# Which engine sends for the bias tables in the second mixer: GpSimd, or SyncE between its weight loads

## The chip, the cores and the metric

One core of one Trainium2 chip runs the kernel in one launch. The metric is the device time in microseconds (us), the median of several runs. Five engines work side by side, each in its own program order: TensorE (PE) multiplies, VectorE (DVE), ScalarE (ACT) and GpSimd (POOL) do elementwise work, and SyncE (SP) here only issues DMAs. They wait for one another through semaphores. A DMA is issued by an instruction in one engine's program; the bytes are moved by the core's 16 DMA engines, and the DMA's semaphore rises when they have landed.

## The reference

Two transformer blocks run one after the other on x of 512 tokens by 1024 channels, all float32. The first has causal pooling, a dilated attention and a gated MLP. The second begins with the part that matters here, a mixer with 14 attention heads of three kinds, whose scores get a bias before the softmax:

```python
# differential attention: 4 heads, two score maps each, ALiBi bias
s = jnp.einsum('bqhd,bkhd->bhqk', qb, k).astype(jnp.float32) * scale + bias      # bias = -slope * |qpos - kpos|
# forgetting attention: 6 heads, causal mask only
# chunk attention: 6 heads, a relative-position bias looked up in a table
s = jnp.einsum('bcqhd,bckhd->bchqk', qc, kb).astype(jnp.float32) * (HEAD_DIM ** -0.5) + bias
```

After the mixer come an output projection, a convolution-gated MLP and a gated embedding step.

## The kernel before, in words

Every float32 product is made of three products of rounded parts: hi times hi, lo times hi, hi times lo. For each load of weights ACT therefore writes `w_hi` and POOL or DVE writes `w_lo` from `w_raw`. The buffers `w_raw`, `w_hi` and `w_lo` have two slots; load n goes to the slot of load n-2, so SP issues it once the `w_lo` of load n-2 is complete.

Mixer two works through 11 chunks of the projection: three of two forgetting heads, three of two chunk heads (`chk`), four of one differential head (`d`), one of the differential values (`dv`). A chunk has two loads, so there are 22, numbered 0 to 21 (`load_projection`, L920). A load of a `chk` chunk is 3 DMAs, one of a `d` chunk 4, one of `dv` 1. While the PE projects one chunk, it attends to the chunk before: for each map m (20 maps; 8 to 13 are forgetting heads, 14 to 19 chunk heads, 0 to 7 differential) and each query tile t from 3 down to 0, the PE forms scores ("S", L2506/L2507), DVE adds the table row, takes the maximum and returns the bank (L1876, semaphore `biased`), ACT takes the exponential (L1306), POOL normalises ("N", L1061), PE transposes ("T", L2518), ACT and DVE split the result (L1313, L1957), and PE multiplies by the values ("PV", L2528/L2530). Between these lie, for each chunk and token tile, "sum" (POOL, L991/L992: the inverse root of the sum of squares), "rows" (DVE, L1813/L1820: scale by it, and return the projection's bank), and "turn" (PE transposes of the finished rows, L2470; then ACT L1289 and L1295 and DVE L1831 write the ring of queries and keys). A planner writes all these steps into one order with small shifts for each engine; each engine then keeps its own order (`mx.orders["pool"]`, L1031). The eight PSUM banks are four for projections and four that S, T, PV and turn take in rotation; a step waits until the one four before it in the rotation has been read.

The bias tables: ten of 128x512 float32, 256 KB each, in two buffers `tables[:, i % 2, :]`. Table i with i from 0 to 5 serves map 14+i, tables 6 to 9 serve the pairs of differential maps. Tables 0 and 1 are sent for by POOL at L1176, after its part of the norm between the blocks. Tables 2 to 9 are steps "table" in POOL's order: POOL waits until the last map that read this buffer is done (`biased`) and issues the DMA (L1068). For the first six, half of the last 64 columns has to be set to minus 1e30 by POOL: for i from 2 to 5 this is a step "mask" (L1072), two units of scores after the step "table":

```python
elif kind == "mask":
    i = s[1]
    pool.wait_ge(table_in[i % 2], 16 * (i // 2 + 1))
    pool.memset(tables[0:HD, i % 2, S - HD:S], MASKED).then_inc(table_masked, 1)
```

The order that the planner gives POOL around table 3 (the first number of a sum is its chunk, the second its token tile; of N the map and its tile):

```
... sum(5,0)  TABLE 3  N(16,3)  sum(5,1)  N(16,2)  sum(5,2)  MASK 3  N(16,1)  sum(5,3)  w_lo of load 13  N(16,0)  TABLE 4 ...
```

DVE's `rows(5,3)` waits for POOL's `sum(5,3)`, and PE's two turns of chunk 5 wait for `rows(5,3)`.

Of the kernel before, what the change touches and what calls it, by code (L numbers as in the profile page):

```python
# [55 lines left out]
def round_done(j, k=SEVEN):  # L56


    return SEVEN * j + (k - 2)
# [270 lines left out]
def two_blocks_kernel(nc, A, out):  # L330
# [23 lines left out]
    G_MIX2 = G_DOWN1 + T * N_DOWN  # L354
# [10 lines left out]
    mixers = []  # L365
    for b, (cnt, steps, chunks, units, c0, norm) in enumerate(((n1, steps1, chunks1, units1, 0, 0),
                                                               (n2, steps2, chunks2, units2, C_MIX2, 2))):
        m = Mixer()
# [9 lines left out]
        for k, chunk in enumerate(chunks):  # L378
            for half in range(1 if chunk[0] == "pool" else 2):
                m.load_at[k, half] = len(m.loads)  # L380
                m.loads.append((k, KH * half, KB if chunk[0] == "pool" else KH))
                last = ("poolproj", k, 1, POOL_PARTS - 1) if chunk[0] == "pool" else ("proj", k, half, T - 1)
# [86 lines left out]
    def table_of_map(m):  # L469

        return 6 + m // 2 if m < 8 else None if m < 14 else m - 14
# [13 lines left out]
    with ExitStack() as ctx:  # L485
# [3 lines left out]
        def sem(name):  # L489
            return ctx.enter_context(nc.semaphore(name))  # L490
# [34 lines left out]
        def at(name, kib, shape, dt=F32):  # L525

            assert kib * KIB + int(np.prod(shape[1:])) * 4 <= arena_kib * KIB, name
            return nc.alloc_sbuf_tensor_at(name, shape, dt, offset=arena_start + int(kib * KIB))
# [57 lines left out]
        tables = at("tables", 44, [P, 2, S])  # L586
# [7 lines left out]
        table_in = [sem("table_in0"), sem("table_in1")]  # L594
# [7 lines left out]
        products_done = sem("products_done")  # L602
# [24 lines left out]
        biased = sem("biased")  # L627
# [175 lines left out]
        def projection_weights(mx, n):  # L803

            k, kb0, kbs = mx.loads[n]
            slot, wide = (mx.c0 + n) % 2, width(mx.chunks[k])
            return [w[:, slot, 0:kbs * wide].rearrange("p (k n) -> p k n", n=wide) for w in (w_raw, w_hi, w_lo)]
# [47 lines left out]
        def _(sp):  # L855
# [26 lines left out]
            def out_chunks(w, c0, b):  # L882
                for j, c in enumerate(OUT_ORDER[b]):
                    load(c0 + j, (c0 + j) % 2, rows(w)[c], rows=True)
# [35 lines left out]
            def load_projection(mx, n):  # L920
                c, (k, kb0, kbs) = mx.c0 + n, mx.loads[n]
                w = A["w_in_2" if mx.b else "w_in"][0].rearrange("(k p) n -> p k n", p=P)[:, kb0:kb0 + kbs, :]
                dst = projection_weights(mx, n)[0]
                if c >= 2:
                    sp.wait_ge(lo_done, 4 * (c - 1))
                at_ = 0
                for col, wide in columns(mx.chunks[k]):
                    sp.dma_start(dst[:, :, at_:at_ + wide], w[:, :, col:col + wide]).then_inc(raw_in[c % 2], 16)
                    at_ += wide

            def const(dst, src, **kw):
                sp.dma_start(dst, src, **kw).then_inc(const_in, 16)

# [20 lines left out]
            for n in range(2, len(mixers[0].loads)):  # L954
# [2 lines left out]
            blocks(A["w_gate"][0], A["w_up"][0])  # L957
            row_chunks(A["w_down"][0], C_DOWN1,
                       [[(piece_lo, round_done(N_BLOCK - 2 + e)), (w_sums, 4 * (N_BLOCK - 1 + e))] for e in range(2)])
            for n in range(len(mixers[1].loads)):  # L960
                load_projection(mixers[1], n)
            out_chunks(A["w_out_2"][0], C_OUT2, 1)
            mixed_pairs(A["w_up_2"][0], C_UP2)
            row_chunks(A["w_down_2"][0], C_DOWN2, [[(gate_w_lo, gate_pieces_done(N_MIXED - 1, 3))], [(val_w_lo, 4 * N_MIXED)]])
# [16 lines left out]
        def _(pool):  # L981
# [8 lines left out]
            def rstd(out_, mean):  # L990
                link(pool.tensor_scalar(mean, mean, EPS, None, ALU.add))  # L991
                return pool.tensor_tensor(out_, mean, half_neg[:, 0:out_.shape[-1]], ALU.pow)  # L992
# [36 lines left out]
            def mixer(mx):  # L1029
                own_n, own_d = mx.cnt.of[mx.steps[0]]["N"], 0  # L1030
                for s in mx.orders["pool"]:  # L1031
                    kind, of = s[0], mx.cnt.of[s]
                    own_n, own_d = own_n + (kind == "N"), own_d + (kind == "pool_d")
                    if kind == "split_lo":
                        weights_lo(mx, s[1], s[2])
                    elif kind == "sum":
                        r = of["sum"]
                        pool.wait_ge(ss_done, r + 1)
                        rstd(qk_rs[:, r % 4, :], qk_ss[:, r % 4, :]).then_inc(rs_done, 1)
                    elif kind == "combine":  # L1040
                        pool.wait_ge(combine_ss, s[1] + 1)
                        pool.tensor_tensor(rs_c[:, :], den_c[:, :], half_neg[:, :], ALU.pow).then_inc(combine_rs, 1)
                    elif kind == "zeros":
                        pool.wait_ge(h_turned, T * (mx.norm + 1))
                        pool.wait_ge(x_squared, T * (mx.norm + 1))
                        for half in range(2):
                            for i in range(2):
                                ins = pool.memset(ring[:, 6 * half + 3 * i + 2, :].bitcast(F32), 0.0)
                        ins.then_inc(zeros_set, 1)
                    elif kind == "N2":  # L1050
                        h, t = s[1:]
                        u, col = mx.unit[2 * h, t], sum_column(h, t)
                        ratio = rden[:, u % 8:u % 8 + 1]
                        pool.wait_ge(second_rden, of["N2"] + 1)
                        pool.tensor_scalar(ratio, ratio, den_d[:, col:col + 1], lam[:, 2:3], ALU.mult, ALU.mult)\
                            .then_inc(ratio_done, 1)
                    elif kind == "N":
                        u, kn = mx.unit[s[1:]], P * (s[2] + 1)
                        pool.wait_ge(rden_done, of["N"] + 1)
                        p = prob[:, u % NPROB, 0:kn]  # L1060
                        pool.tensor_tensor(p, p, rden[:, u % 8:u % 8 + 1].to_broadcast([P, kn]), ALU.mult)\  # L1061
                            .then_inc(normed, 1)
                    elif kind == "table":
                        i = s[1]
                        last = max(mx.unit[m, 0] for m in range(20) if table_of_map(m) == i - 2)
                        pool.wait_ge(biased, last + 1)
                        table = A["rel_table"][:, i, :] if i < 6 else A["alibi"][:, i - 6, :]
                        pool.dma_start(tables[:, i % 2, :], table).then_inc(table_in[i % 2], 16)  # L1068
                    elif kind == "mask":
                        i = s[1]  # L1070
                        pool.wait_ge(table_in[i % 2], 16 * (i // 2 + 1))
                        pool.memset(tables[0:HD, i % 2, S - HD:S], MASKED).then_inc(table_masked, 1)  # L1072
                    elif kind in ("widen", "mean", "pool_d"):
                        m = s[1]
                        u, d, spare = pool_u[:, m, :], pool_d[:, m, :], (pool_d[:, 1, :], pool_u[:, 0, :])[m]
                        if kind == "widen":
                            j = s[2]
                            dst, src = (spare, d)[j % 2], (u, spare, d, spare)[j]
                            if j == 0:
                                k = mx.chunks.index(("pool",))  # L1080
                                pool.wait_ge(bank_read, mx.cnt.of["poolproj", k, m, POOL_PARTS - 1]["bank"] + 1)
                                if m:
                                    pool.wait_ge(pool_out, m)
                            sh = 1 << j
                            link(pool.tensor_copy(dst[:, 0:sh], src[:, 0:sh]))
                            link(pool.tensor_tensor(dst[:, sh:S], src[:, sh:S], src[:, 0:S - sh], ALU.add))
                        elif kind == "mean":
                            lo, win = HD * s[2], 2 << (2 * m + s[2])
                            src = (spare, d)[s[2]]
                            pool.wait_ge(normed, own_n)  # L1090
                            if own_d:
                                pool.wait_ge(pool_out, own_d)
                            pool.wait_ge(lo_done, lo_split[0])
                            link(pool.tensor_tensor(d[lo:lo + HD, 0:16], src[lo:lo + HD, 0:16],
                                                    pool_inv[lo:lo + HD, m, :], ALU.mult))
                            link(pool.tensor_scalar(d[lo:lo + HD, 16:S], src[lo:lo + HD, 16:S], 1.0 / win, None, ALU.mult))
                        else:
                            pool.tensor_tensor(d, d, u, ALU.subtract).then_inc(pool_out, 1)
# [73 lines left out]
                    block_sums(2 * i + e, e)  # L1172
            norm(2, True)

            for i in range(2):
                pool.dma_start(tables[:, i, :], A["rel_table"][:, i, :]).then_inc(table_in[i], 16)  # L1176
            pool.dma_start(causal[:, :], A["causal"]).then_inc(causal_in, 16)
            pool.memset(ft[:, :].bitcast(F32), 0.0).then_inc(ft_zeroed, 1)
            pool.memset(ones[:, :], 1.0)
# [1673 lines left out]
```

## Time and profile before

| | us |
|---|---|
| median of 3 runs | 1303.28 (1303.08 to 1303.86) |
| the profiled execution, its own time | 1302.76 |
| its span, first to last instruction | 1301.0 |
| PE busy | 1279.9 (98%) |
| DVE / ACT / POOL busy | 863.7 / 682.8 / 474.9 |

The span is what the trace covers; the profiled execution's time is 1.76 us more. Busy time is the sum of instruction durations. The idle time before an instruction, and what released it, stand in brackets at its end in the timelines. Mixer two lies between about 577 and 850 us of the span.

### The profile page before, as it was taken

What the parts mean: (1) busy time and instruction counts of PE and PEld (TensorE: products, weight loads), DVE (VectorE), ACT (ScalarE), POOL (GpSimd) and SP (SyncE); (2) the same over time, 40 slices, a digit from 0 to 9 for tenths busy, and PEclk for the clock granted to TensorE, in tenths of its full rate; (3) what the DMA queues carried; (4) which work ended last, traced back from release to release, by engine and by line L of the source; (5) the groups of instructions that cost most, each with busy time, mean ns of one, the idle gap of its engine ahead of it and who ended that gap; (6) DMA issues with size and microseconds to landing.
All of it is one profiled execution on the core that took longest, in us unless ns stands there. A gap on an engine that the chain in (4) does not pass through costs nothing. (4 is left out here: it accounts for less than half of the span.)

```text
span 1301.0 us, 21929 instructions
## 1 busy us (share of the span) xinstructions
PE 1279.9 (98%) x7792; PEld 1162.3 (89%) x7792; DVE 863.7 (66%) x1584; ACT 682.8 (52%) x1361; POOL 474.9 (37%) x546
## 2 busy tenths in 40 slices
PE   8999999999999999999999999999999999999998
PEld 6999988999999988889999988889888989888887
DVE  4677766799888733374666778557977777633454
ACT  4666745445555522256667678435455546422352
POOL 5565681256555300027766756210122232000000
PEclk9999999999999999999999999999999999999999
DMA  6312213233322332223222332232223232422221
GB/s 195 87 52 80 90 42 129 77 119 108 119 97 97 119 108 97 89 62 86 74 65 50 72 68 89 91 115 83 97 82 114 81 113 65 172 95 97 72 98 65
DMA packets 120639, 120.64 MB, mean 93 GB/s; under 512 B 22732, under 2 KB 107419, under 8 KB 120562
## 3 DMA queue, kind: packets, MB, share of 16 engines
q1 hardware_dynamic: 118464, 112.92, 27.5%
q0 software_dynamic: 2096, 6.71, 1.6%
q8 instruction: 46, 0.75, 0.2%
q14 instruction: 31, 0.25, 0.1%
q10 hardware_dynamic: 2, 0.00, 0.0%
HBM read 117.52 MB, written 2.10 MB: 92 GB/s over the span
## 5 line engine op out<-in xcount | busy, mean ns | idle before, releaser
L2337 PE MATMUL ps<-h_hi,w_hi 128*128 128x256 f32 (+1 forms) x752 | 239.1, 318 | 0.4 <-ACT ps L1578 0.4
L2338 PE MATMUL ps<-h_lo,w_hi 128*128 128x256 f32 (+1 forms) x752 | 238.5, 317 | 0.0
L2339 PE MATMUL ps<-h_hi,w_lo 128*128 128x256 f32 (+1 forms) x752 | 238.3, 317 | 0.0
L1714 DVE TENSOR_TENSOR w_lo<-w_raw,w_hi 128x512 fp32r<-128x512 f32 x164 | 105.8, 692 | 143.5 <-ACT w_hi L1217 143.4
L1217 ACT ACTIVATE w_hi<-w_raw 128x512 fp32r<-128x512 f32 x164 | 92.4, 620 | 176.7 <-PE ps L2560 153.3
L2556 PE MATMUL ps<-w_hi,st_hi 128*128 128x512 f32 x432 | 169.1, 391 | 0.0
L2423 PE MATMUL ps<-w_hi,h_hi 128*128 128x384 f32 (+2 forms) x528 | 167.9, 328 | 0.6 <-DVE work L1813 0.3
L2560 PE MATMUL ps<-w_hi,st_lo 128*128 128x512 f32 x432 | 168.2, 389 | 0.0
L2558 PE MATMUL ps<-w_lo,st_hi 128*128 128x512 f32 x432 | 168.2, 389 | 0.0
L2425 PE MATMUL ps<-w_hi,h_lo 128*128 128x384 f32 (+2 forms) x528 | 163.3, 319 | 0.0
L2339 PEld LDWEIGHTS ps<-h_hi,w_lo 128*128 128x128 f32 x752 | 143.3, 191 | 9.6
L2337 PEld LDWEIGHTS ps<-h_hi,w_hi 128*128 128x128 f32 x752 | 143.3, 191 | 9.5 <-ACT ps L1578 0.6
L2338 PEld LDWEIGHTS ps<-h_lo,w_hi 128*128 128x128 f32 x752 | 143.4, 191 | 8.5
L1026 POOL TENSOR_TENSOR w_lo<-w_raw,w_hi 128x384 fp32r<-128x384 f32 (+2 forms) x116 | 115.8, 1018 | 48.7 <-ACT w_hi L1229 45.8
L2430 PE MATMUL ps<-w_lo,h_hi 128*128 128x384 f32 (+2 forms) x528 | 105.0, 320 | 0.5 <-POOL w_lo L1026 0.5
L2423 PEld LDWEIGHTS ps<-w_hi,h_hi 128*128 128x128 f32 x528 | 99.5, 188 | 3.1 <-issue 1.1
L2425 PEld LDWEIGHTS ps<-w_hi,h_lo 128*128 128x128 f32 x528 | 99.7, 189 | 0.8
L2337 PE MATMUL ps<-t_hi,w_hi 128*128 128x256 f32 x344 | 97.5, 283 | 1.8 <-DVE hid L2064 0.9
L2339 PE MATMUL ps<-t_hi,w_lo 128*128 128x256 f32 x344 | 97.4, 283 | 0.0
L2338 PE MATMUL ps<-t_lo,w_hi 128*128 128x256 f32 x344 | 97.3, 283 | 0.0
L2560 PEld LDWEIGHTS ps<-w_hi,st_lo 128*128 128x128 f32 x432 | 81.1, 188 | 16.9
L2556 PEld LDWEIGHTS ps<-w_hi,st_hi 128*128 128x128 f32 x432 | 81.1, 188 | 16.8 <-DVE h_lo L1751 0.3
(264 smaller groups left out, 2899.3 us busy)
## 6 DMA issues: line engine op xcount, KB each, us to landing
w_raw<-in_w_up_dram SPq DMA_DIRECT2D x25, 1024.0 KB, 5.2
w_raw<-in_w_down_dram SPq DMA_DIRECT2D x22, 1024.0 KB, 4.8
w_raw<-in_w_in_dram SPq DMA_DIRECT2D x72, 256.0 KB, 3.4
w_raw<-in_w_gate_dram SPq DMA_DIRECT2D x11, 1024.0 KB, 5.2
w_raw<-in_w_out_dram SPq DMA_DIRECT2D x8, 1024.0 KB, 4.8
w_raw<-in_w_up_dram SPq DMA_DIRECT2D x16, 512.0 KB, 3.5
w_raw<-in_w_in_dram SPq DMA_DIRECT2D x32, 128.0 KB, 2.9
w_raw<-in_w_ple_gate_dram SPq DMA_DIRECT2D x4, 1024.0 KB, 5.0
```

The costliest lines, as they stand in the source:

```text
L1026: pool.tensor_tensor(w_lo[:, c % 2, q], w_raw[:, c % 2, q], w_hi[:, c % 2, q].bitcast(F32), ALU.subtract)\
L1217: act.activation(w_hi[:, slot, q], w_raw[:, slot, q], ACT.Copy).then_inc(hi_done, 1)
L1714: dve.tensor_tensor(w_lo[:, slot, q], w_raw[:, slot, q], w_hi[:, slot, q].bitcast(F32), ALU.subtract).then_inc(lo_done, 1)
L2337: pe.matmul(out_, s_hi, m_hi, start=first and n == 0, stop=False, skip_group_check=True)
L2338: pe.matmul(out_, s_hi, m_lo, start=False, stop=False, skip_group_check=True)
L2339: mm = pe.matmul(out_, s_lo, m_hi, start=False, stop=last and n == len(pairs) - 1, skip_group_check=True)
L2423: pe.matmul(bank, h_hi[:, kb0 + i, tok], hi[:, i, :], start=half == 0 and i == 0, stop=False, skip_group_check=True)
L2425: pe.matmul(bank, h_lo[:, kb0 + i, tok], hi[:, i, :], start=False, stop=False, skip_group_check=True)
L2430: mm = pe.matmul(bank, h_hi[:, kb0 + i, tok], lo[:, i, :], start=False, stop=half == 1 and i == KH - 1, skip_group_check=True)
L2556: pe.matmul(bank, rows_hi[:, k, tok], hi[:, k, col], start=first and k == 0, stop=False, skip_group_check=True)
L2558: pe.matmul(bank, rows_hi[:, k, tok], lo[:, k, col], start=False, stop=False, skip_group_check=True)
L2560: mm = pe.matmul(bank, rows_lo[:, k, tok], hi[:, k, col], start=False, stop=last and k == RB - 1, skip_group_check=True)
```

## The change

The ten DMAs for the tables leave POOL's program and go into SP's. A new function `loads_and_tables` writes one order for SP out of POOL's order: load 0, load 1, table 0, table 1, load 2, load 3, and then, walking through POOL's steps, each table where POOL had it, and each load n where POOL begins the last of its own pieces of `w_lo` of load n-2. Written out this gives: loads 4 to 13, T2, load 14, T3, load 15, T4, load 16, T5, load 17, T6, load 18, T7, load 19, load 20, T8, load 21, T9, and then the loads of the output projection. Tables 0 and 1 now wait on SP for the last product of block one (`products_done`, `G_MIX2`), the others for the same counts of `biased` as before. The masks, their place and their waits stay on POOL.

```diff
+            def loads_and_tables(mx):
+                order = [("load", 0), ("load", 1), ("table", 0), ("table", 1), ("load", 2), ("load", 3)]
+                for s in mx.orders["pool"]:
+                    if s[0] == "table":
+                        order.append(s)
+                    elif s[0] == "split_lo" and s[2] == (1 if ("split_rest", s[1], 1) in mx.cnt.of else 3) \
+                            and 2 <= s[1] < len(mx.loads) - 2:
+                        order.append(("load", s[1] + 2))
+                return order
+
+            def load_table(mx, i):
+                if i < 2:
+                    sp.wait_ge(products_done, G_MIX2)
+                else:
+                    last = max(mx.unit[m, 0] for m in range(20) if table_of_map(m) == i - 2)
+                    sp.wait_ge(biased, last + 1)
+                table = A["rel_table"][:, i, :] if i < 6 else A["alibi"][:, i - 6, :]
+                sp.dma_start(tables[:, i % 2, :], table).then_inc(table_in[i % 2], 16)
...
-            for n in range(len(mixers[1].loads)):
-                load_projection(mixers[1], n)
+            for kind, n in loads_and_tables(mixers[1]):
+                if kind == "load":
+                    load_projection(mixers[1], n)
+                else:
+                    load_table(mixers[1], n)
...
-                    elif kind == "table":
-                        i = s[1]
-                        last = max(mx.unit[m, 0] for m in range(20) if table_of_map(m) == i - 2)
-                        pool.wait_ge(biased, last + 1)
-                        table = A["rel_table"][:, i, :] if i < 6 else A["alibi"][:, i - 6, :]
-                        pool.dma_start(tables[:, i % 2, :], table).then_inc(table_in[i % 2], 16)
...
-            for i in range(2):
-                pool.dma_start(tables[:, i, :], A["rel_table"][:, i, :]).then_inc(table_in[i], 16)
```

## Rows read from the trace of the kernel before

**Rows 1.** The page: busy time, share and instructions of each engine, and the span.

```profile
span 1301.0 us, 21929 instructions
...
PE 1279.9 (98%) x7792; PEld 1162.3 (89%) x7792; DVE 863.7 (66%) x1584; ACT 682.8 (52%) x1361; POOL 474.9 (37%) x546
```

**Rows 2.** PE by stretches: length, PE busy (instructions), clock, DMA share, GB/s.

```profile
700.00:722.00 22.00, 21.52 (x136) 1.00 0.19 48
722.00:742.00 20.00, 18.41 (x141) 1.00 0.31 67
742.00:840.00 98.00, 93.95 (x701) 1.00 0.31 90
sum 250.00, PE 242.63; mean PE 60.66
```

**Rows 3.** Instructions on the tile tables: duration min/median/max ns, starts; time to landing.

```profile
L1068 POOL DMA_DIRECT2D tables<-in_rel_table_dram x4: 622/626/639, 706.1 to 743.9; - x4
L1176 POOL DMA_DIRECT2D tables<-in_rel_table_dram x2: 538/586/633, 586.1 to 586.8; - x2
...
DMA to landing us min/median/max: 3.1/3.4/4.3
```

**Rows 4.** SP's issues of projection loads in order of time: start, length, count.

```profile
574.20 1.47 SPq L928 DMA_DIRECT2D w_raw<-in_w_in_dram  x3
...
706.21 2.88 SPq L928 DMA_DIRECT2D w_raw<-in_w_in_dram  x4
722.01 2.92 SPq L928 DMA_DIRECT2D w_raw<-in_w_in_dram  x4
731.67 2.02 SPq L928 DMA_DIRECT2D w_raw<-in_w_in_dram  x4
744.13 2.06 SPq L928 DMA_DIRECT2D w_raw<-in_w_in_dram  x4
```

**Rows 5.** Line 928 from 700 to 800 us: its issues' durations, and time to landing.

```profile
L928 SPq DMA_DIRECT2D w_raw<-in_w_in_dram x30: 367/507/1412, 706.2 to 793.5; - x30
...
DMA to landing us min/median/max: 2.3/3.0/3.8
```

**Rows 6.** POOL in order of time around tables 2 to 5 and their masks.

```profile
713.95 0.14 POOL L1072 MEMSET tables<- 64x64 f32 x1
...
718.19 0.63 POOL L1068 DMA_DIRECT2D tables<-in_rel_table_dram  x1
...
724.71 1.04 POOL L992 TENSOR_TENSOR qk_rs<-qk_ss,half_neg 128x4 f32<-128x4 f32 x1
725.70 0.14 POOL L1072 MEMSET tables<- 64x64 f32 x1
...
726.82 1.04 POOL L992 TENSOR_TENSOR qk_rs<-qk_ss,half_neg 128x4 f32<-128x4 f32 x1
...
738.25 0.14 POOL L1072 MEMSET tables<- 64x64 f32 x1
...
749.28 0.14 POOL L1072 MEMSET tables<- 64x64 f32 x1
```

**Rows 7.** DVE in order of time, from rows(5,3) to the last ring of chunk 5.

```profile
727.96 0.42 DVE L1813 TENSOR_TENSOR work<-ps,qk_rs 128x256 f32<-128x256 f32 x1 [0.55 <-POOL qk_rs L992]
...
728.50 0.68 DVE L1876 CUSTOM_DVE_ANT_0 prob<-ps,tables 128x512 f32<-128x512 f32 x1
...
734.35 1.51 DVE L1831 SCALAR_TENSOR_TENSOR ring<-ps,gcol,ring 64x512 fp32r<-64x512 f32 x2 [1.21 <-ACT ring L1289]
```

**Rows 8.** ACT in the same stretch.

```profile
730.01 0.71 ACT L1306 ACTIVATE prob<-prob,neg_max 128x512 f32<-128x512 f32 x1
730.62 0.19 ACT L1306 ACTIVATION_READ_ACCUMULATOR prob<-prob,neg_max 128x1 f32 x1
730.84 1.39 ACT L1289 ACTIVATE ring<-ps,gcol 64x512 fp32r<-64x512 f32 x2
```

**Rows 9.** PE: the turns of chunk 5, and the wait for their ring.

```profile
729.31 1.25 PE L2470 MATMUL ps<-ident,work 128*128 128x128 f32 x8
...
735.92 0.38 PE L2506 MATMUL ps<-ring 128*128 128x256 f32 x1 [1.59 <-DVE ring L1831]
```

**Rows 10.** The start of mixer two: PE's last product of block one; ACT's split of load 2.

```profile
577.48 0.39 PE L2560 MATMUL ps<-w_hi,st_lo 128*128 128x512 f32 x1
...
594.31 1.58 ACT L1229 ACTIVATE w_hi<-w_raw 128x768 fp32r<-128x768 f32 x2 [2.93 <-PE ps L2430]
```

**Rows 11.** From 700 to 840 us, PE's and DVE's waits: total us, times, longest.

```profile
PE ps L2470 <- DVE neg_max L1876: 1.7, 3, 0.6
...
DVE w_lo L1911 <- POOL w_lo L1026: 3.2, 3, 2.0
...
DVE work L1813 <- POOL qk_rs L992: 1.6, 3, 0.6
```

**Rows 12.** Around table 9: the last read of its buffer (DVE), SP's next load.

```profile
800.10 0.29 DVE L1876 CUSTOM_DVE_ANT_0 prob<-ps,tables 128x128 f32<-128x128 f32 x1
...
803.21 0.37 SPq L861 DMA_DIRECT2D w_raw<-in_w_out_dram  x1
```

## The prediction

> **What bounds the kernel now.** I read the page first. PE is busy for 1279.9 of 1301.0 us, POOL for 37% [rows 1]; so an instruction taken off POOL is worth something only where PE stands still because POOL is late. Second, PE by stretches over mixer two: from 590 to 840 us it is busy 242.63 of 250 us, so 7.4 us stand still, and 1.59 of them between 722 and 742 [rows 2]. Third, PE's waits from 700 to 840 us, where tables 2 to 9 are sent for. None names POOL. The largest kind with a pattern, 1.7 us in three pieces, is a turn that waits for DVE to return a bank [rows 11]. DVE for its part waits for POOL, 1.6 us for inverse roots and 3.2 us for `w_lo` [rows 11]. That is the only road by which a faster POOL could reach PE, and equally the road by which a late POOL reaches it. Fourth, the instructions on the tables, which give the price on POOL and the time to landing [rows 3]. Last, SP's issues in order of time [rows 4], because the change makes each table wait behind a load.
>
> **The change part by part.**
>
> *POOL loses ten issues.* Eight at L1068 of 0.626 us make 5.0 us, two at L1176 make 1.17 us [rows 3]. They lie beside other work. The two early ones are followed by POOL work that DVE's first sums do not wait for; of the eight, only DVE's 4.8 us of waits for POOL could shrink [rows 11], and PE's own waits in that stretch name DVE's bank returns and rings, not anything that POOL is late with. Bounds for PE: nothing, or at most the 1.6 us of waits for inverse roots. I take nothing.
>
> *SP gains ten issues.* One DMA takes 0.37 to 0.51 us to issue there [rows 5]. The next load starts at least 7 us after a projection load's issues end (724.93 to 731.67 is the shortest of the gaps in [rows 4]), so they fit. I take nothing.
>
> *SP gains ten waits; what is queued behind each?* Tables 0 and 1 wait for the last product of block one, which ends at 577.87 [rows 10]. Load 2 stood at 574.20 [rows 4] and now follows them: 577.9 plus two issues of 0.5 is 578.9, 4.7 us later; with 1.5 us of issues and 3.8 us to land it is there by 584.2. ACT reads it at 594.31, and is held there by PE [rows 10]: 10 us of cover. Tables 2 to 7 wait for `biased` counts that are reached well before the load ahead of them in the queue has gone. Table 9 waits for the unit that DVE finishes at 800.10 plus 0.29; the load behind it goes at 803.21 [rows 12], so 2.4 us of cover after the issue. All at nothing.
>
> *The tables come at another time.* This is where I find a price. The new order puts table i behind a load whose own wait may end later than POOL's turn for that table:
>
> - Table 2: behind load 13, whose issues end at 706.21 + 2.88 = 709.09 [rows 4]. Landing at 3.1 us, the least of the tables' rows [rows 3], is 712.2, at 3.8 us [rows 5] 712.9. POOL's mask stands at 713.95 [rows 6]: hidden by 1.0 us.
> - Table 3: POOL sent for it at 718.19 [rows 6]. Load 14, now ahead of it, waits until 722.01 and its four issues end at 724.93 [rows 4]. The table is issued 6.7 us later than before, and lands at 724.93 + 3.1 = 728.03. POOL comes to its mask at 725.70 [rows 6]. It now waits until about 728.05: **2.35 us late**.
> - Table 4: behind load 15, 731.67 + 2.02 = 733.69 [rows 4], landed by 736.8 to 737.5, mask at 738.25 [rows 6]: hidden by 0.8 us. The delay below moves both sides by similar amounts.
> - Table 5: behind load 16, 744.13 + 2.06 = 746.19 [rows 4], landed by 749.3 to 750.0, mask at 749.28 [rows 6], or 0.6 us sooner without POOL's issue: POOL stands for 0.6 to 1.3 us. Behind this mask come only a normalisation and `w_lo` pieces of load 15, which are needed several steps later, and no "sum"; the sum of the last tile is ahead of it in POOL's order. I take nothing, at most 0.5.
> - Tables 6 to 9 have no mask, and each is sent for many units of scores before its first use. Nothing.
>
> *Table 3's 2.35 us, followed on.* Behind the mask on POOL are N(16,1) and sum(5,3), whose root ended at 726.82 + 1.04 = 727.86 and will end at 730.2 [rows 6]. DVE's rows(5,3) at 727.96 had already waited 0.55 us for it [rows 7], so DVE is late by the whole 2.35 us: rows(5,3) ends at 730.7, and PE's turn, at 729.31 before [rows 9], starts 1.4 us late. DVE next adds the table for S(17,3), now from 730.85 to 731.53 instead of 728.50 to 729.18 [rows 7]. ACT's exponential waits for it, so 730.01 becomes 731.55. Exponential and accumulator took until 730.81, and ACT began the ring at 730.84 [rows 8]; now that is 732.38, 1.54 us later. The ring is ACT's and then DVE's chain (DVE had waited 1.21 us for ACT in it [rows 7]), and PE's S(17,1) at 735.92 had stood 1.59 us for its end [rows 9]. So the wait is not cover: it is the end of the same chain, and PE resumes 1.54 us later. Roughly, PE loses the mask's delay less 0.8 us.
>
> **The sum.** 8 + 2 issues off POOL: 0. SP's waits: 0. Table 3: +1.5. The span becomes 1302.5, and that execution's time 1302.76 + 1.5 = 1304.3. The median of the runs shown is 0.5 us above the profiled time, so I forecast 1303.28 + 1.5 = 1304.8. PE has almost no later gaps in which to win it back.
>
> Bounds of the unknown, the landing of a table issued by SP, which this trace does not have: 2.3 us, the least of L928 [rows 5], gives a mask delay of 1.55 and a loss of 0.75; 4.3 us, the most of the tables [rows 3], gives 3.55 and 2.75. I take 3.1, the same bytes at the nearest shape. Load 14's issues, too, had one of 1.4 us where 0.5 is usual [rows 4, 5]; if that hiccup goes, 0.9 us comes off.
>
> The rows show 3.1 us to landing even for a table that POOL sent for [rows 3]. The Trainium skill, "DMA: Bandwidth & Descriptors", section "Latency and other measured facts", puts the first byte at about 0.6 us for a DMA from the synchronising engine and about 1 us for one from GpSimd. By that the table would land 0.4 us sooner after its issue, and the loss would be about 1.1 instead of 1.5; no row here sets the two paths side by side for the same transfer. The same page, section "Two DMAs through the same engine are not ordered", says that descriptors within one queue start in order. That speaks against this change, since the table now stands in the same queue behind the load; its estimate would be a landing toward the upper end above.
>
> **The rivals.**
>
> *Hidden after all.* Table 3 lands before or hardly after POOL's mask. It needs a landing by about 726.5 (loss = delay less 0.8 us). For it: the 1.4 us issue in load 14 may not recur, and 2.3 us have been seen [rows 5]; together 724.0 + 2.3 = 726.3. Against: both must hold. Time 1303.3, from 1302.8 to 1303.8.
>
> *Slower by more than 0.2%.* One mechanism: table 3, in one queue behind four DMAs of load 14, lands late. The loss passes 2.6 us when the landing comes after 729.1, that is 4.2 us after the issue. For it: the tables' own worst is 4.3 [rows 3]. Against: in this stretch load DMAs, which also stand behind their siblings, landed in 2.3 to 3.8 us [rows 5]. At 5 us the time is 1303.3 + 3.4 = 1306.7.
>
> *Faster.* POOL's 0.63 us per table reach PE through DVE's waits. For it: DVE waits 4.8 us for POOL [rows 11]. Against: PE's waits name none of it, and the turns that wait 1.7 us wait for a bank return whose chain starts at PE's own transposes. At its most this wins 1.6 us and costs table 3's loss; to pass 2.6 us nearly all of the 4.0 us that PE stands still from 742 to 840 [rows 2] would have to go. 1300.5 at best.
>
> **How the numbers follow.** The forecast's mechanism with a loss of 0.5 to 2.6 us: 0.59. Hidden: 0.17. Slower by more than 2.6 us: 0.20. Faster by more than 2.6 us: 0.04. 0.2% is 2.6 us, about what a measurement of this kernel tells from no change, so same is 0.59 + 0.17 = 0.76. The range reaches from 1302.7, just under the hidden case, to 1307.0, just above a landing of 5 us; outside I leave about 0.15.
>
> **What would show it.** Right: POOL's mask of table 3 (L1072) idle for 1.5 to 3 us on a DMA of `tables`, the next root late by as much, DVE's L1813 behind it waiting 2 to 3 us for POOL, and PE between 722 and 742 us standing 2.5 to 4 us instead of 1.59. The masks of tables 2 and 4 don't wait. Load 2 goes at about 579 and nobody waits for it. Wrong: that mask doesn't wait; or another does, before a "sum"; or a load is held by a table's `biased` wait and ACT stands for `w_raw`; or the three waits of 0.55 us at L2470 shrink.

## The result, and the profile after

| | before | changed |
|---|---|---|
| median of 17 runs each, us | 1303.32 (1302.57 to 1304.49) | 1305.75 (1304.79 to 1309.69) |
| profiled execution, span, us | 1301.0 | 1304.4 |
| ratio | | 1.0019, 95% interval 1.0013 to 1.0026 |

The change costs 2.4 us by the medians, 1.7 to 3.4 us by the interval. That is inside the predicted range. The ratio of 1.0019 is just inside 0.2%, though its interval reaches beyond; the forecast was 1304.8.

Granted clock and PE's busy time by stretches, in the profile of the changed kernel, against [rows 2] (length, PE busy with its count, clock, DMA share, GB/s):

```profile
700.00:722.00 22.00, 21.52 (x136) 1.00 0.16 37
722.00:742.00 20.00, 17.30 (x121) 0.91 0.35 80
742.00:840.00 98.00, 94.56 (x709) 1.00 0.31 90
```

The idle time is where it was expected: 2.70 us instead of 1.59 between 722 and 742. And there is something that was not expected: the granted clock, 1.00 everywhere in [rows 2], is 0.91 in that stretch. That is why the idle time grows by only 1.1 us while the span grows by more: products at a lower clock take longer and count as busy.

SP in order of time around table 3, against [rows 4]:

```profile
722.82 2.88 SPq L928 DMA_DIRECT2D w_raw<-in_w_in_dram  x4
725.75 0.50 SPq L950 DMA_DIRECT2D tables<-in_rel_table_dram  x1
```

Load 14 goes 0.81 us later than before. This whole profile is shifted by 0.81 us from its first products on, 700 us ahead of table 3: four products took 1.62 us at the start (below) where the same four took 0.95 in the profile of before. The profiles of the experiments are shifted by 0.0 to 1.4 us in the same way, and two profiles of one and the same kernel (each table ahead of its load, below) by 0.0 and by 1.4 us, so this belongs to the execution. Readings "net of the shift" have it taken off.

```profile
11.73 1.62 PE L2408 MATMUL ps<-w_hi,h_hi 128*128 128x384 f32 x4
```

POOL, against [rows 6], masks of tables 2, 3, 4 and 5:

```profile
714.77 0.14 POOL L1090 MEMSET tables<- 64x64 f32 x1
...
729.41 0.14 POOL L1090 MEMSET tables<- 64x64 f32 x1 [2.86 <-DMA tables<-in_rel_table_dram]
...
730.53 1.04 POOL L1016 TENSOR_TENSOR qk_rs<-qk_ss,half_neg 128x4 f32<-128x4 f32 x1
...
741.17 0.14 POOL L1090 MEMSET tables<- 64x64 f32 x1
...
752.82 0.14 POOL L1090 MEMSET tables<- 64x64 f32 x1 [0.94 <-ACT w_hi L1245]
```

Masks 2 and 4 don't wait, mask 3 waits 2.86 us for its table, mask 5 waits 0.94 us. (The releaser named for mask 5 is ACT's; the instruction waits for nothing but the table's semaphore.) Net of the 0.81 us, mask 3 stands at 728.60 instead of 725.70: 2.9 us late. Then DVE, against [rows 7], and ACT, against [rows 8]:

```profile
731.66 0.42 DVE L1829 TENSOR_TENSOR work<-ps,qk_rs 128x256 f32<-128x256 f32 x1 [3.46 <-POOL qk_rs L1016]
...
737.27 1.51 DVE L1847 SCALAR_TENSOR_TENSOR ring<-ps,gcol,ring 64x512 fp32r<-64x512 f32 x2 [0.86 <-ACT ring L1305]
```

```profile
732.93 0.72 ACT L1322 ACTIVATE prob<-prob,neg_max 128x512 f32<-128x512 f32 x1 [2.01 <-DVE neg_max L1892]
733.56 0.19 ACT L1322 ACTIVATION_READ_ACCUMULATOR prob<-prob,neg_max 128x1 f32 x1
733.77 1.39 ACT L1305 ACTIVATE ring<-ps,gcol 64x512 fp32r<-64x512 f32 x2
```

ACT begins the ring at 733.77 instead of 730.84, 2.1 us late net of the shift. Last PE, against [rows 9]; its second product on the ring, at 739.33, has no idle time ahead of it any more:

```profile
732.34 0.66 PE L2486 MATMUL ps<-ident,work 128*128 128x128 f32 x4 [2.05 <-DVE vs L1836]
733.64 0.98 PE L2486 MATMUL ps<-ident,work 128*128 128x128 f32 x4 [0.64 <-DVE pt_lo L1973]
...
739.33 0.36 PE L2522 MATMUL ps<-ring 128*128 128x256 f32 x1
```

From there to the end the two executions run in step: 3.4 us of difference in the span, less the 0.81 of the start, is 2.6 us, all of it made between 729 and 739 us. Of this, 2.1 us is the late chain: DVE ends the ring at 737.27 + 1.51 = 738.78, which is 2.1 us later than before, net of the shift. The other 0.5 us is PE's own: in the kernel before, PE took the ring up 0.06 us after its end; here it is still busy with earlier products and begins 0.55 us after it. One more view, PE in single microseconds of the changed kernel, shows the clock:

```profile
732.00:733.00 1.00, 0.66 (x4) 1.00 0.00 0
733.00:734.00 1.00, 0.36 (x3) 0.89 0.00 0
734.00:735.00 1.00, 1.00 (x6) 0.50 0.00 0
735.00:736.00 1.00, 1.00 (x7) 0.50 0.00 0
736.00:737.00 1.00, 1.00 (x7) 0.50 0.82 162
737.00:738.00 1.00, 1.00 (x8) 0.91 0.87 148
```

After PE has stood 2.05 and 0.64 us, it gets the lower of its two levels (1.2 instead of 2.4 GHz) for 3.4 us (from 733.78 to 737.18 in finer slices). The pause ends at the turn, but products go on at half speed behind it, and that is what keeps PE busy past the end of the ring.

### The profile page after: what moved, and what is told of

Read it like the earlier page. It is cut to its first block and busy times, and to the rows that moved or that the text cites. A ratio compares the mean times of both kernels' runs of the same rounds, so it can differ in the third digit from the quotient of the medians.

```text
span 1304.4 us, 21929 instructions
## 1 busy us (share of the span) xinstructions
PE 1282.1 (98%) x7792; PEld 1165.0 (89%) x7792; DVE 863.7 (66%) x1584; ACT 683.0 (52%) x1361; POOL 469.0 (36%) x536
```

## Experiments

Theory A: the whole loss is table 3, which reaches its mask late; what stands behind the mask on POOL, sum(5,3), carries it to DVE's rows, ACT's ring and PE. Rival B: the loss is spread over SP's ten new issues and waits, or comes of having tables and weights in one DMA queue. Rival C: POOL's freed time is worth something. The comparisons with before come from the same chip.

**Table 3 alone on SP.** The kernel before, with this in SP's order and nine tables left on POOL (table 3 gets a semaphore of its own in this and the next kernel):

```diff
+                    if s[0] == "table":
+                        if s[1] == 3:
+                            order.append(s)
...
-                    elif kind == "table":
+                    elif kind == "table" and s[1] != 3:
```

> The kernel before with table 3 alone moved to SP, behind load 14; the nine others stay on POOL. Theory A (table 3 is late at its mask, and its delay runs through sum(5,3), rows(5,3) and the turn to PE): the whole loss is here, +2.0 to +2.9 us against before, POOL's mask of table 3 waits 2.5 to 3 us, and the granted clock dips once right after PE's wait. Rival B (the loss is spread: ten more issues and waits on SP, the tables in one DMA queue with the weights, or the start of the program): under +1 us.

Measured: 1306.02 us (1304.94 to 1309.47, six runs), before 1303.10, ratio 1.0030 (1.0018 to 1.0042). In its profile the mask waits as in the changed kernel:

```profile
728.63 0.14 POOL L1098 MEMSET tables<- 64x64 f32 x1 [2.73 <-DMA tables<-in_rel_table_dram]
```

One table of ten makes the whole loss.

**All tables but table 3 on SP.** The reverse of the edit above (`s[1] != 3` in SP's order, `s[1] == 3` on POOL).

> The changed kernel with table 3 alone given back to POOL, at its old place. Theory A: equal to before, within 0.5 us, PE's waits from 722 to 742 us back at 1.6 us, granted clock 1.000. Rival B: +1.5 to +2.5 us, as in the changed kernel.

Measured: 1303.17 us (1302.65 to 1306.04), before 1303.10, ratio 1.0004 (0.9995 to 1.0013). PE between 722 and 742 us is back to [rows 2]:

```profile
722.00:742.00 20.00, 18.41 (x140) 1.00 0.31 67
```

Nine issues and nine waits on SP cost nothing in this profile (span 1301.1 with a shift of 0.15 us; before 1301.0), and by the runs' interval at most 1.7 us. Mask 3 stands at 725.85, unhindered. Rival B falls.

**Each table ahead of the load that DVE releases.**

```diff
-                    elif s[0] == "split_lo" and s[2] == (1 if ("split_rest", s[1], 1) in mx.cnt.of else 3) \
+                    elif s[0] in ("split_lo", "split_rest") \
+                            and s == (("split_rest", s[1], 1) if ("split_rest", s[1], 1) in mx.cnt.of else ("split_lo", s[1], 3)) \
                             and 2 <= s[1] < len(mx.loads) - 2:
```

> All ten tables on SP, but each ahead of the load whose own wait ends later: the place of a load that DVE releases is DVE's step, not POOL's. Order: T2, T3, L14, T4, L15, T5, L16 and so on. Theory A: the loss is gone, the time is before's within 0.5 us, perhaps 0.3 us less by the issues taken off POOL. Rival B: still +1.5 us or more, since nothing is taken off SP. Rival C (POOL's freed time is worth something once no table is late): 1 us or more below before.

Measured: 1303.05 us (1302.17 to 1307.12), before 1303.10, ratio 1.0004 (0.9995 to 1.0013). Table 3 is now sent 7 us ahead of load 14. SP in order of time, tables 3 and 4 with the loads between and behind them:

```profile
714.84 0.34 SPq L951 DMA_DIRECT2D tables<-in_rel_table_dram  x1
721.99 3.04 SPq L928 DMA_DIRECT2D w_raw<-in_w_in_dram  x4
...
726.68 0.34 SPq L951 DMA_DIRECT2D tables<-in_rel_table_dram  x1
731.65 2.02 SPq L928 DMA_DIRECT2D w_raw<-in_w_in_dram  x4
```

So SP can send for all ten tables without a loss that shows: the profiled span is 1301.1 us, and the interval allows 1.7 us at most. It wins nothing either, which answers rival C. DVE's waits for POOL from 700 to 840 us shrink only from the 1.6 and 3.2 us of [rows 11]:

```profile
DVE w_lo L1928 <- POOL w_lo L1051: 2.9, 3, 2.0
...
DVE work L1830 <- POOL qk_rs L1017: 1.2, 3, 0.6
```

and PE's longest kinds of wait are unchanged (2.1 and 1.7 us). The tables land a little sooner after their issue than when POOL sent for them: 2.6 to 2.7 us for tables 3 to 5, against 3.1 to 3.5 us in the profile of before.

**The same once more.** Two of its eleven runs lay 3.5 to 4 us above the rest.

> All tables on SP, each ahead of the load that DVE releases, once more: two of its eleven runs lay 3.5 to 4 us above the rest. If that belongs to this order, two or three of the new runs lie there again; if it is a rare event of any of these kernels, none or one. The median is expected within 0.5 us of before's.

Measured: 1303.77 us (1302.59 to 1307.30), before 1303.24, ratio 1.0004 (0.9995 to 1.0013); one run of eleven was high. Three of 22 here, one of eleven in each of two kernels near before's time (1306.04 and 1307.31 us), and one of before's own (1306.72 us): these kernels all have such runs. Together that is 5 of 44 with tables on SP against 1 of 91 of the kernel before, so they may well be commoner with the tables on SP. All but the one at 1306.04 us have a mean granted clock of 0.997, against 0.999 or 1.000 in the other runs taken with them. No such run was profiled, and what makes them stays open.

**PE kept busy in its wait.** The changed kernel with products whose results are thrown away:

```diff
+                        if (mx.b, k, j) == (1, 5, 0):
+                            bank = own_bank(mx, s)
+                            for _ in range(8):
+                                pe.matmul(ps[:, bank, :], h_hi[:, 0, 0:P], h_hi[:, 1, :], start=True, stop=True)
                         pe.wait_ge(bank_read, mx.cnt.of["rows", k, T - 1]["bank"] + 1)
```

> The changed kernel, with 8 products of 512 columns (1.8 us) put on PE ahead of its wait for rows(5,3), into the bank that the turn then overwrites; the extra products are thrown away. They lie in the 2.05 us that PE stands still there. Theory A with a share for the clock (PE's wait itself costs 2.1 us, the 3.4 us at the lower clock after it another 0.5): the dip goes, granted clock 1.000, and the time is 0.3 to 0.8 us below the changed kernel's. Rival (the dip costs nothing, it lies inside the chain over ACT and DVE): the same time as the changed kernel. Rival (the clock does not answer to this wait): the dip stays.

Measured: 1305.39 us (1304.29 to 1305.93) in eleven runs. The changed kernel had 1305.75 in its first 17 runs and 1305.58 on another chip, so the difference is at the low end of what was expected and no more than the medians scatter. The clock says more. Its mean as granted is 1.000 in all eleven runs, where the changed kernel had 0.998 or less in 15 of its 17. In the profile the table is as late as in the changed kernel, the products fill the wait, the clock stays at 1.00, and PE waits for the ring again:

```profile
729.56 2.06 PE L2486 MATMUL ps<-h_hi 128*128 128x512 f32 x8
731.63 0.66 PE L2490 MATMUL ps<-ident,work 128*128 128x128 f32 x4
732.93 0.63 PE L2490 MATMUL ps<-ident,work 128*128 128x128 f32 x4 [0.64 <-DVE pt_lo L1973]
...
738.14 0.39 PE L2526 MATMUL ps<-ring 128*128 128x256 f32 x1 [0.82 <-DVE ring L1847]
```

**The mask behind sum(5,3).** The changed kernel, one step moved in POOL's order:

```diff
+    if diff_maps:
+        pool_order = orders["pool"]
+        pool_order.remove(("mask", 3))
+        pool_order.insert(pool_order.index(("sum", 5, 3)) + 1, ("mask", 3))
```

> The changed kernel with one step moved in POOL's order: the mask of table 3 comes after sum(5,3) instead of before N(16,1) and sum(5,3). The table lands as late as before. If what costs is what stands behind the mask on POOL (sum(5,3), and so rows(5,3) and the turn), the loss goes: the mask still waits about 1 us, DVE waits for it some 0.3 us, PE loses 0 to 0.3 us, the time is before's within 0.5 us. If the late table itself costs, or the traffic, the loss of 2 us stays.

Measured: 1303.49 us (1302.52 to 1307.31), before 1303.39, ratio 1.0005 (0.9996 to 1.0014). Table 3 is sent at 724.97, as late as ever, and the loss is gone. (It landed some 0.7 us sooner than in the changed kernel, still 2.2 us after the old place of the mask.) POOL in order of time:

```profile
725.82 0.61 POOL L1089 TENSOR_TENSOR prob<-prob,rden 128x256 f32<-128x256 f32 x1
726.51 0.23 POOL L1019 TENSOR_SCALAR qk_ss<-qk_ss 128x4 f32<-128x4 f32 x1
726.83 1.04 POOL L1020 TENSOR_TENSOR qk_rs<-qk_ss,half_neg 128x4 f32<-128x4 f32 x1
728.05 0.14 POOL L1094 MEMSET tables<- 64x64 f32 x1 [0.19 <-DMA tables<-in_rel_table_dram]
```

The late table costs nothing that shows by itself; what costs is the work that stood behind its mask.

**Sooner and later.** The changed kernel with table 3 between the second and third DMA of load 14:

```diff
                     at_ += wide
+                    if mx.b and n == 14 and at_ == 2 * wide:
+                        load_table(mx, 3)
```

> The changed kernel with table 3 sent between the second and the third DMA of load 14, so about 1.1 us sooner. By loss = delay of the mask less 0.8 us: mask late by 1.7 us, loss 0.9 us, with no dip of the granted clock or a smaller one. If the loss is a step (late or not late), 2 us as in the changed kernel.

Measured: 1304.15 us (1303.48 to 1305.70), before 1303.39, ratio 1.0006 (0.9997 to 1.0015). The profiled execution was the slowest of the eleven, so it does not stand for the median. The loss by the medians, 0.76 us, is near the 0.9 us expected; the profile's, below, is not. Nine of the eleven runs have a mean granted clock of 1.000; the profiled one has 0.999 and a stretch at the lower clock.

And with two small DMAs ahead of table 3:

```diff
+                if i == 3:
+                    for h in range(2):
+                        sp.dma_start(spare[:, 48 * h:48 * h + 48], A["rel_table"][:, 0, 0:48]).then_inc(spare_in, 16)
```

> The changed kernel with two small DMAs (into a tile that nobody reads) issued on SP right before table 3, so that it is sent about 1.0 us later. By the same rule: mask late by 3.8 us, loss 3.0 us, and more where the granted clock falls in PE's wait. If the loss is a step, 2 us.

Measured: 1306.53 us (1305.96 to 1308.88), before 1303.39, ratio 1.0027 (1.0017 to 1.0037).

**The changed kernel on the same chip.**

> The changed kernel itself once more, on the chip of the three others, as the mark to read them by: +2.0 to +2.6 us against before, one stretch of 3.4 us at the lower clock after PE's wait, and now and then a run 3 us above the rest.

Measured: 1305.58 us (1305.09 to 1307.17), before 1303.39, ratio 1.0018 (1.0009 to 1.0027). The stretch at the lower clock was expected, and this profile has none, though PE stood still for 1.51 and 0.64 us; the mean clock is 0.998 in six of the eleven runs. PE between 722 and 742 us, and its product on the ring, which waits for it as in the kernel before:

```profile
722.00:742.00 20.00, 17.05 (x130) 1.00 0.34 80
...
738.63 0.39 PE L2522 MATMUL ps<-ring 128*128 128x256 f32 x1 [0.81 <-DVE ring L1847]
```

By medians, with table 3 sent sooner, as in the change, and later: +0.76, +2.19, +3.14 us. The intervals of neighbours overlap, those of the first and the last don't. So the loss grows with the lateness and is no step. The six profiles in which mask 3 waits with sum(5,3) behind it allow a check of "loss = delay less 0.8 us". The shift is load 14's issue less 722.01; the delay is mask 3's start less the shift less 725.70; the loss is the span less 1301.0 less the shift:

| profile | shift | delay of mask 3 | delay less 0.8 | loss | left over | lower clock behind the wait |
|---|---|---|---|---|---|---|
| filler | 0.25 | 2.75 | 1.95 | 1.95 | 0.0 | no |
| changed, second chip | 1.14 | 2.35 | 1.55 | 1.56 | 0.0 | no |
| table 3 alone | 0.17 | 2.76 | 1.96 | 2.03 | 0.1 | yes |
| changed | 0.81 | 2.90 | 2.10 | 2.59 | 0.5 | yes |
| table 3 later | 0.87 | 3.25 | 2.45 | 2.93 | 0.5 | yes |
| table 3 sooner | 0.97 | 2.21 | 1.41 | 2.03 | 0.6 | yes |

The lateness in the kernels with table 3 sooner and later came out as 2.2 and 3.25 us where 1.7 and 3.8 were expected. Sooner: the issue moved by only 0.6 us, net of the shifts, instead of 1.1. Later: the issue moved by 0.9 us, but the table landed 3.0 us after it instead of 3.6. The spans are known to 0.1 us, and within that the rule holds in the two profiles without a stretch at the lower clock, the "dip". With it there are 0.1 to 0.6 us more. PE shows where they come from: with the dip it begins its product on the ring 0.53 to 0.56 us after DVE has ended it (changed, later, sooner), and in the two profiles without it, and with table 3 alone, 0.05 or 0.06 us after. In the two without it PE had stood 0.8 us there, so a dip costs only what it delays PE beyond those 0.8 us. (With table 3 sooner this explains 0.5 of the 0.6 us; the rest is open.) With table 3 alone it began 1.6 us earlier against the work (731.56 against 733.78, shifts of 0.17 and 0.81 taken off) and was over before PE needed the ring:

```profile
731.00:732.00 1.00, 0.43 (x2) 0.78 0.00 0
732.00:733.00 1.00, 0.82 (x5) 0.50 0.00 0
733.00:734.00 1.00, 1.00 (x6) 0.50 0.25 37
734.00:735.00 1.00, 1.00 (x6) 0.51 0.58 213
735.00:736.00 1.00, 1.00 (x12) 1.00 0.58 116
```

## Why the prediction was right, point by point

- **Where PE could be reached.** Right: the way from POOL to PE led through DVE, and a loss came along it, not a gain. POOL's ten issues were costed at nothing; the order with every table ahead of its load has them off POOL and its ratio is 1.0004 (0.9995 to 1.0013). The 4.8 us given as DVE's waits for POOL left out two kinds, of 1.8 and 0.5 us; both are unchanged in that order, so nothing hung on them. And the shortest gap between SP's loads is 6.7 us, not "at least 7"; the issues fitted all the same.
- **SP's issues and waits at nothing.** Right for nine tables together, by the kernel that leaves table 3 on POOL. The first two tables moved load 2 as worked out, to 579.55 us in a profile shifted by 0.81 (forecast 578.9).
- **Tables 2, 4 and 5.** Right: no wait at masks 2 and 4, and 0.94 us at mask 5, foreseen as 0.6 to 1.3, with no loss on PE behind it.
- **Table 3.** The step is right by four experiments: alone it makes the loss, without it there is none, ahead of load 14 it is gone, and so it is with the mask behind sum(5,3).
- **Its size.** In the first profile of the changed kernel two terms of the sum were too small. The landing was taken as 3.1 us and was 3.6 (issued at 725.75, mask at 729.41), which made the delay 2.9 instead of 2.35 and the loss 2.1 instead of 1.54. And the price of PE standing still was taken to be only that time; the lower clock behind it added 0.5 us. 1.54 + 0.55 + 0.5 is 2.6, the loss of that profile; the medians say 2.4. In the second profile of the same kernel both terms are as forecast: the landing took 3.2 us, the delay was 2.35 us, the loss 1.56 us, and the clock stayed up. Even so its execution took 1305.55 us, about the median, since its shift at the start is one of the largest, 1.14 us. How the 0.9 us by which the medians lie above the forecast divides among landing, clock and shift is therefore not known. The times of the runs don't settle it: on the second chip the six runs at a mean clock of 0.998 have a median of 1305.40 us, the five at 0.999 or 1.000 one of 1305.89.
- **What the Trainium skill states.** The Trainium skill, "DMA: Bandwidth & Descriptors", section "Latency and other measured facts", led to a landing sooner by 0.4 us when SP issues. Behind four load DMAs table 3 landed after 3.0 to 3.6 us in the six profiles that have it there, POOL's took 3.1 us for the same table, so no gain shows; ahead of load 14 it landed after 2.6 and 2.7 us, which agrees with the figure. For the start order named in the same page of the Trainium skill, section "Two DMAs through the same engine are not ordered", the profiles give no proof: the order with table 3 ahead of load 14 also puts it into a quieter stretch. That section gives no time, so the landing "toward the upper end" was the prediction's own reading of it.
- **PE at the turns.** One wait was left out: the second turn of chunk 5 waits for the bank that DVE returns with `pt_lo`, 0.64 us. It lies inside ACT's chain, so it cost nothing.
- **The rivals.** "Slower by more than 0.2%" names the right mechanism, and the result came close to it: 2.4 us with a boundary at 2.6 and an interval of 1.7 to 3.4. That the result stayed on the near side of the boundary is in part luck, since the sum had 1.5. "Hidden after all" would have needed a landing before 726.5, and it came at 728.6 net of the shift. "Faster" fell.

## What to carry to other kernels

A DMA that moves to another queue takes on the waits of whatever is ahead of it there. Before merging two orders, read for each transfer when its predecessor is really released (here a load released by DVE's last piece, not by POOL's), not where a planner lists it. If it then lands late, ask what stands behind the instruction that waits for it: here a mask that nobody needed for another 2.8 us held back an inverse root (the "sum") that DVE was already waiting for, and moving the mask by two steps was as good as sending the table 10 us sooner.

## What the runs showed that was not expected

In four of the five profiles in which PE stood still for the late table, a wait of 1.37 to 2.41 us with a second of 0.18 to 0.65 behind it came with 3.4 us at the lower clock; in the fifth, waits of 1.51 and 0.64 us were followed by none. Since 1.37 and 0.64 us were followed by a dip and 1.51 and 0.64 us were not, the length of the waits alone doesn't decide it, and what does stays open. By the mean clock of the runs (0.998 or less) such a stretch is common in the changed kernel, 21 of 28 runs, and was seen in none of the eleven with eight products laid into the wait and in one of 74 of the kernel before that the experiments took. It cost between nothing and 0.5 us on PE's way to the ring, by where it fell against the next wait. A pause of PE in this kernel can thus cost a little more than the lateness that caused it, and by an amount that changes from run to run.
